# Down projections of three groups as seven half-size products for each pair of output tiles

## The reference

```python
h = rms_norm(x, g_mlp[layer])
x = x + jnp.square(jax.nn.relu(h @ w_up[layer])) @ w_down[layer]
```

## Time and profile before

| | us |
|---|---|
| median of 3 runs | 1569.56 (1568.65 to 1571.38) |
| the profiled execution | 1571.89 |
| its span | 1570.2 |
| TensorE busy | 1517.2 (97%) |
| VectorE busy | 726.8 (46%) |
| ScalarE busy | 491.9 (31%) |
| granted clock of TensorE, mean | 0.989 of 2.4 GHz |

### The profile page before, as it was taken

How to read it: one execution, slowest core, us unless ns; L and a number is a source line. 1 busy time by engine, 2 the same in 40 slices (tenths; PEclk the granted TensorE clock), 3 DMA queues, 4 the chain that set the end, 5 groups by cost and what they waited for, 6 DMA issues and landing times.

```text
span 1570.2 us, 33444 instructions
## 1 busy us (share of the span) xinstructions
PE 1517.2 (97%) x13119; PEld 1423.2 (91%) x13119; DVE 726.8 (46%) x1265; ACT 491.9 (31%) x787; POOL 117.8 (8%) x238
## 2 busy tenths in 40 slices
PE   6999999989999999999999999898999999999996
PEld 5999867679999999999999996666999999999996
DVE  4355475635443343333543466764544434334333
ACT  5111254423332131221321116442333313213133
POOL 5310112310000000000010000222000000000000
PEclk9999999999999999999999999999999999999998
DMA  4322577732223222232242237775223222322222
GB/s 132 98 80 79 151 245 251 257 101 82 79 80 94 80 80 82 79 94 81 80 136 80 82 101 238 241 236 163 75 81 87 81 83 78 94 80 81 83 79 74
DMA packets 230949, 178.84 MB, mean 114 GB/s; under 512 B 9320, under 2 KB 202924, under 8 KB 230850
## 3 DMA queue, kind: packets, MB, share of 16 engines
q1 hardware_dynamic: 217154, 137.50, 29.9%
q0 software_dynamic: 13696, 40.00, 8.0%
HBM read 170.20 MB, written 7.26 MB: 113 GB/s over the span
## 4 chain that ended last, share of the span: by engine, by line
PE 91%; DVE 3%; SPq 2%; issue 1%; DMA 1%; ACT 1%; POOLq 0%; POOL 0%; ACTq 0%; DVEq 0%
PE B L1301 70%; PE B L1518 4%; PE B L1530 3%; PE B L1327 2%; PE B L1612 2%; PE B L1574 1%; PE B L1318 1%; PE B L1550 1%; PE B L1561 1%; SPq L382 1%; DMA WR<-in_w_in_even_dram 1%; DVE SK L1194 1%; PE B L1596 1%; PE B L1528 1%; PE B L1400 1%
## 5 line engine op out<-in xcount | busy, mean ns | idle before, releaser
L554 ACT ACTIVATE WH<-WR 128x1024 fp32r<-128x1024 f32 x175 | 184.3, 1053 | 435.1 <-PE B L1301 422.3
L822 DVE TENSOR_TENSOR WL<-WR,WH 128x1024 fp32r<-128x1024 f32 x188 | 230.2, 1224 | 57.8 <-ACT WH L544 29.0
L1301 PE MATMUL B<-ffH,WH 128*128 128x288 f32 x1024 | 219.7, 295 | 0.0
L1301 PE MATMUL B<-ffL,WH 128*128 128x288 f32 x1024 | 218.0, 294 | 0.0
L1301 PE MATMUL B<-ffH,WL 128*128 128x288 f32 x1024 | 217.5, 293 | 0.0
L1301 PE MATMUL B<-H2H,WH 128*128 128x288 f32 x960 | 205.7, 294 | 0.0
L1301 PE MATMUL B<-H2L,WH 128*128 128x288 f32 x960 | 204.2, 294 | 0.0
L1301 PE MATMUL B<-H2H,WL 128*128 128x288 f32 x960 | 203.8, 293 | 0.0
L1301 PE MATMUL B<-HH,WH 128*128 128x288 f32 x832 | 179.4, 297 | 4.1 <-DVE WL L822 2.6
L1301 PE MATMUL B<-HH,WL 128*128 128x288 f32 x832 | 178.1, 296 | 0.0
L856 DVE TENSOR_TENSOR X<-B,X 128x288 f32 (+1 forms) x160 | 65.9, 453 | 242.4 <-PE B L1301 242.1
(11 more groups left out here) (297 smaller groups left out, 1692.4 us busy)
## 6 DMA issues: line engine op xcount, KB each, us to landing
WR<-in_w_up_dram SPq DMA_DIRECT2D x64, 512.0 KB, 4.1
WR<-in_w_down_dram SPq DMA_DIRECT2D x64, 512.0 KB, 3.7
KRX<-in_cache_fox_k_dram SPq DMA_DIRECT2D x48, 256.0 KB, 4.2
WR<-in_w_in_odd_dram SPq DMA_DIRECT2D x24, 512.0 KB, 3.7
...
```

The source lines that it names most:

```text
L554: A(WH[1 - u][:], WR[1 - u][:], ACT.Copy).then_inc(S["w_high"], 1)
L822: V.tensor_tensor(WL[u][:], WR[u][:], WH[u][:].bitcast(F32), ALU.subtract).then_inc(S["w_low"], 1)
L1301: last = M(B[2 * u + h][:, 0:TH], w[u][:, k, :], x[:, k, h * TH:(h + 1) * TH], start=(k == 0 and n == 0), stop=(k == KT - 1 and n == 2))
```

## The change

The hidden tiles of groups 0, 1 and 2 are no longer kept as ffH and ffL. The down projection of such a group goes over NQ=4 pairs of output tiles. A pair's product is a 2x2 block product: blocks of weights by output tile m and parity e of the k tile (a11, a12, a21, a22, each [128, 4, 128]), blocks of activations by parity of the hidden tile and half of the tokens. It is made of seven block products instead of eight (Winograd's form): of weights a11, a12, a22 and the sums S1 = a21+a22, S2 = S1-a11, S4 = a12-S2, S3 = a11-a21, with the activation blocks 11, 21, 22 and the differences T1, T2, T3, T4. Each product is 4 k tiles x 3 terms = 12 matmuls of 288 columns into one bank, of all eight in turn, and is added with its operand broadcast to one, two, three or four quarters of the pair's two tiles of X.

- The order becomes up 0, seven 0, up 1, seven 1, up 2, seven 2, up 3, down 3. The loops over down units of groups 0 to 2 are gone.
- `evac_ops` evacuates an up unit to FR; an odd unit (u=1) also makes T2, T3, T4, an even one T1; ScalarE copies to OPH, VectorE subtracts to OPL.
- SP loads the weights of a pair (1 MB) into ZR or WRP by turns; ZR, ZH, ZL, ZS lie on HH and HL, WRP on WR[0] and WR[1].
- For each pair ScalarE makes seven ZH (`block_high`) and VectorE four sums (`weight_sum`), seven ZL (`block_low`) and seven additions (`add_product`). Pair 0's are put among the last two up units, the others among the additions of the pair before.
- The first unit of down 3 waits for the last hidden tile only ahead of its last k tile (`late_chunk_unit`).
- Several semaphores are merged (f_ln, tok_scale, state_turned and others); this is left out below, as are empty lines. Indents are reduced within a piece.

```diff
+OPH = place("OPH", [P, 7, KT // 2, TH], F32R, arena)
+OPL = place("OPL", [P, 7, KT // 2, TH], F32R, arena + 14 * KT * TH)
+FR = place("FR", [P, 8, TH], F32, arena + 28 * KT * TH)
+ZH = place("ZH", [P, 7, KT // 2, P], F32R, h_addr)
+ZL = place("ZL", [P, 7, KT // 2, P], F32R, h_addr + 14 * KT * P)
+ZS = place("ZS", [P, 7, KT // 2, P], F32, h_addr + 14 * KT * P)
+ZR = place("ZR", [P, KT, 2 * P], F32, h_addr + 28 * KT * P)
+WRP = place("WRP", [P, KT, 2 * P], F32, wr_addr)
+SC = place("SC", [P, 2, KT // 2, P], F32, tmp_addr)
...
+MLP_ORDER = [("up", 0), ("seven", 0), ("up", 1), ("seven", 1), ("up", 2), ("seven", 2), ("up", 3), ("down", 3)]
+NQ = KT // 2
+OP_T1, OP_11, OP_21, OP_22, OP_T2, OP_T3, OP_T4 = range(7)
+FR_T1, FR_11, FR_12, FR_21, FR_22, FR_T2, FR_T3, FR_T4 = range(8)
+PRODUCTS = [("11", OP_11), ("S1", OP_T1), ("12", OP_21), ("S2", OP_T2), ("S4", OP_22), ("S3", OP_T3), ("22", OP_T4)]
+SUM_NO = {"S1": 1, "S2": 2, "S4": 3, "S3": 4}
+def pair_no(L, grp, q):
+    return (L * (FG - 1) + grp) * NQ + q
+def product_bank(q, i):
+    return B[(4 + 7 * q + i) % 8]
...
+def block_src(Q, i):
+    name = PRODUCTS[i][0]
+    if name in ("S1", "S2"):
+        return SC[:, int(name[1]) - 1]
+    if name in ("S3", "S4"):
+        return ZS[:, i]
+    return raw_block(Q, int(name[0]) - 1, int(name[1]) - 1)
+def up_loop(eng, body, g0, i0, turns):
+    with eng.Fori(0, turns) as it:
+        for u in range(2):
+            body(it * 2 + (g0 + u), it * 2 + (i0 + u), it + i0 // 2, u, "next")
...
+if kind == "seven":
+    for q in range(NQ):
+        Q = pair_no(L, grp, q)
+        if q == 0 and grp == 0:
+            sp.wait_ge(S["unit_done"], G_OUT[L] + KT + 1)
+        if q == 1:
+            sp.wait_ge(S["w_low"], g + 2)
+        if Q >= 2:
+            sp.wait_ge(S["block_low"], 7 * (Q - 1))
+        sp.dma_start((ZR if q % 2 == 0 else WRP)[:, :, :], dn_v[L][grp][:, :, 2 * P * q:2 * P * (q + 1)]
+                     ).then_inc(S[f"pair_in{q % 2}"], 16)
+    sp.wait_ge(S["block_low"], 7 * (pair_no(L, grp, NQ - 1) + 1))
+    continue
...
+def evac_ops(L, grp):
+    m0 = L * FG * KT + grp * KT
+    j0 = pair_no(L, grp, 0)
+    def body(g, i, j, u, more):
+        next_high(g, u, more)
+        act.wait_ge(S["relu_scaled"], i + (m0 + 1))
+        raw = FR[:, FR_11:FR_12 + 1] if u == 0 else FR[:, FR_21:FR_22 + 1]
+        A(raw, raw, ACT.Square).then_inc(S["relu_squared"], 1)
+        if u == 1:
+            act.wait_ge(S["relu_squared"], i + (m0 + 1))
+            A(OPH[:, OP_21:OP_22 + 1, ds(j, 1), :].rearrange("p s o t -> p (s o) t"), raw, ACT.Copy).then_inc(S["op_high"], 1)
+        act.wait_ge(S["op_sums"], j * 3 + (3 * j0 + 1 + 2 * u))
+        lo, hi, f = (OP_T1, OP_11, FR_T1) if u == 0 else (OP_T2, OP_T4, FR_T2)
+        A(OPH[:, lo:hi + 1, ds(j, 1), :].rearrange("p s o t -> p (s o) t"), FR[:, f:f + hi + 1 - lo], ACT.Copy).then_inc(S["op_high"], 1)
+    return body
+def block_high(Q, i):
+    name = PRODUCTS[i][0]
+    if name in SUM_NO:
+        act.wait_ge(S["w_sum"], 4 * Q + SUM_NO[name])
+    else:
+        act.wait_ge(S[f"pair_in{Q % 2}"], 16 * (Q // 2 + 1))
+    if Q >= 1:
+        act.wait_ge(S["product"], 7 * (Q - 1) + i + 1)
+    A(ZH[:, i], block_src(Q, i), ACT.Copy).then_inc(S["block_high"], 1)
...
+if kind == "seven":
+    for q in range(1, NQ):
+        for i in range(7):
+            block_high(pair_no(L, grp, q), i)
+    cut_high(g)
+    continue
+if kind == "down":
     for i in range(KT):
         evac_sq(2 + 2 * L)(g + i, i, i % 2, None if last and i == KT - 1 else "next")
+elif grp == FG - 1:
+    unit_loop(act, evac_up(L, grp), g, KT)
 else:
-    body = evac_up(L, grp) if kind == "up" else evac_none
+    body, Q = evac_ops(L, grp), pair_no(L, grp, 0)
     if n == 0:
         next_high(g, 0, "second")
         norm(1 + 2 * L)
-        body(g, 0, 0, None)
-        body(g + 1, 1, 1, None)
+        body(g, 0, 0, 0, None)
+        body(g + 1, 1, 0, 1, None)
     first = 2 if n == 0 else 0
-    unit_loop(act, body, g + first, KT - first, i0=first)
+    up_loop(act, body, g + first, first, (KT - 2 - first) // 2)
+    block_high(Q, 0)
+    block_high(Q, 1)
+    body(g + KT - 2, KT - 2, NQ - 1, 0, "next")
+    for i in range(2, 5):
+        block_high(Q, i)
+    body(g + KT - 1, KT - 1, NQ - 1, 1, None)
+    block_high(Q, 5)
+    block_high(Q, 6)
...
+def evac_ops(L, grp, b0=0, z=None):
+    m0 = L * FG * KT + grp * KT
+    j0 = pair_no(L, grp, 0)
+    def body(g, i, j, u, more):
+        next_low(g, u, more)
+        if z is not None and u == 0:
+            norm(z)
+        dve.wait_ge(S["unit_done"], g + 2)
+        f0 = FR_11 if u == 0 else FR_21
+        for h in range(2):
+            done = V.scalar_tensor_tensor(FR[:, f0 + h], B[b0 + 2 * u + h][:, 0:TH], 0.0, R[:, h * TH:(h + 1) * TH], ALU.max, ALU.mult)
+        done.then_inc(S["relu_scaled"], 1)
+        dve.wait_ge(S["relu_squared"], i + (m0 + 1))
+        if u == 0:
+            V.tensor_tensor(FR[:, FR_T1], FR[:, FR_12], FR[:, FR_11], ALU.subtract).then_inc(S["op_sums"], 1)
+        else:
+            V.tensor_tensor(FR[:, FR_T2], FR[:, FR_22], FR[:, FR_T1], ALU.subtract).then_inc(S["op_sums"], 1)
+            V.tensor_tensor(FR[:, FR_T3], FR[:, FR_22], FR[:, FR_12], ALU.subtract)
+            dve.wait_ge(S["op_sums"], j * 3 + (3 * j0 + 2))
+            V.tensor_tensor(FR[:, FR_T4], FR[:, FR_21], FR[:, FR_T2], ALU.subtract).then_inc(S["op_sums"], 1)
+            low_ops(OP_21, OP_22, FR_21, j, j * 3 + (3 * j0 + 2)).then_inc(S["op_half"], 1)
+        lo, hi, f = (OP_T1, OP_11, FR_T1) if u == 0 else (OP_T2, OP_T4, FR_T2)
+        low_ops(lo, hi, f, j, j * 3 + (3 * j0 + (1 if u == 0 else 3))).then_inc(S["evac_dve"], 1)
+    return body
+def low_ops(lo, hi, f, j, made):
+    dve.wait_ge(S["op_high"], made)
+    return V.tensor_tensor(OPL[:, lo:hi + 1, ds(j, 1), :].rearrange("p s o t -> p (s o) t"), FR[:, f:f + hi + 1 - lo],
+                           OPH[:, lo:hi + 1, ds(j, 1), :].rearrange("p s o t -> p (s o) t").bitcast(F32), ALU.subtract)
+def block_low(Q, i):
+    dve.wait_ge(S["block_high"], 7 * Q + i + 1)
+    V.tensor_tensor(ZL[:, i], block_src(Q, i), ZH[:, i].bitcast(F32), ALU.subtract).then_inc(S["block_low"], 1)
+def weight_sum(Q, q, name):
+    a11, a12, a21, a22 = (raw_block(Q, m, e) for m in range(2) for e in range(2))
+    out = block_src(Q, [o[0] for o in PRODUCTS].index(name))
+    if name == "S1":
+        dve.wait_ge(S[f"pair_in{q % 2}"], 16 * (Q // 2 + 1))
+        done = V.tensor_tensor(out, a21, a22, ALU.add)
+    elif name == "S2":
+        dve.wait_ge(S["w_sum"], 4 * Q + 1)
+        done = V.tensor_tensor(out, SC[:, 0], a11, ALU.subtract)
+    elif name == "S4":
+        if Q >= 1:
+            dve.wait_ge(S["product"], 7 * (Q - 1) + 5)
+        dve.wait_ge(S["w_sum"], 4 * Q + 2)
+        done = V.tensor_tensor(out, a12, SC[:, 1], ALU.subtract)
+    else:
+        if Q >= 1:
+            dve.wait_ge(S["product"], 7 * (Q - 1) + 6)
+        done = V.tensor_tensor(out, a11, a21, ALU.subtract)
+    done.then_inc(S["w_sum"], 1)
+def add_product(Q, q, i):
+    dve.wait_ge(S["product"], 7 * Q + i + 1)
+    if i > 0:
+        dve.wait_ge(S["product_read"], 7 * Q + i)
+    bank = product_bank(q, i)[:, 0:TH]
+    both = X[:, 2 * q:2 * q + 2, :]
+    if i == 0:
+        x = both.rearrange("p m (h t) -> p m h t", h=2)
+    elif i == 1:
+        x = both[:, :, TH:T]
+    elif i == 3:
+        x = both.rearrange("p m t -> p (m t)")[:, TH:2 * T].rearrange("p (n t) -> p n t", t=TH)
+    elif i == 5:
+        x = X[:, 2 * q + 1, :].rearrange("p (h t) -> p h t", h=2)
+    else:
+        x = {2: X[:, 2 * q, 0:TH], 4: X[:, 2 * q, TH:T], 6: X[:, 2 * q + 1, 0:TH]}[i]
+    if i == 0:
+        bank = bank.unsqueeze(1).unsqueeze(1).broadcast_to([P, 2, 2, TH])
+    elif i in (1, 3, 5):
+        bank = bank.unsqueeze(1).broadcast_to([P, 3 if i == 3 else 2, TH])
+    V.tensor_tensor(x, bank, x, ALU.add).then_inc(S["product_read"], 1)
...
+if kind == "seven":
+    for q in range(NQ):
+        Q = pair_no(L, grp, q)
+        for i in range(7):
+            if q < NQ - 1 and i in (0, 1, 4, 5):
+                weight_sum(Q + 1, q + 1, {0: "S1", 1: "S2", 4: "S4", 5: "S3"}[i])
+            add_product(Q, q, i)
+            if q < NQ - 1:
+                block_low(Q + 1, i)
+            elif i == 5:
+                cut_low(g, 0)
+    continue
+if kind == "down":
     for i in range(KT):
         evac_add(2 + 2 * L)(g + i, i, i % 2, None if last and i == KT - 1 else "next")
+elif grp == FG - 1:
+    unit_loop(dve, evac_up(L, grp), g, KT)
 else:
-    body = evac_up(L, grp) if kind == "up" else evac_add(None)
+    body, Q = evac_ops(L, grp), pair_no(L, grp, 0)
     if n == 0:
         for u in range(2):
-            evac_up(L, grp, 4, 1 + 2 * L)(g + u, u, u, "second" if u == 0 else None)
+            evac_ops(L, grp, 4, 1 + 2 * L)(g + u, u, 0, u, "second" if u == 0 else None)
     first = 2 if n == 0 else 0
-    unit_loop(dve, body, g + first, KT - first, i0=first)
```

(71 more changed lines are left out.)

46 lines of the change are left out of this document (25 added, 21 removed).

## The result

The changed kernel took **1616.01 us** in the median of four runs (1612.59 to 1618.98), against 1570.47 us for the kernel before in the same rounds (1568.65 to 1573.94). The ratio is 1.0285, with a 95% interval of 1.0263 to 1.0307. The profiled span is 1613.8 us, 43.6 us above the one before. The forecast was 1611 us.

A forecast was written before the change was run, and what follows sets the result against it. TensorE was taken to bound the kernel, busy 97% of the span. Waits net of removed matmuls (+21 us) and low clock (+20 us) on the 1569.6 us median gave 1611 us, range 1585 to 1640.

The forecast's parts named there:

- Removed, 38.1 us: Down projections of three groups in two layers: 48 matmuls fewer each, 6 x 6.35 = 38.1 us saved.
- Steps of 0.60 us for 512 elements: VectorE: operations behind one another overlap, so each of 512 elements costs 0.60 us, not its full 0.684.
- rival B: VectorE's pieces take their full duration, 13.6 us for a pair, 28 us more in all: 1639 us; chance 0.10.
- Broadcast PSUM operand at 1.04 ns for an element: VectorE's additions into X: no traced operation had this operand, so the rate of 1.04 ns an element was taken.
- Odd units 0.2 us, first groups 1.1 us: Up units: TensorE waits 0.2 us behind an odd unit, twice a group; 1.1 us in each layer's group 0.
- Last up unit stands 3.9 us: Unit 7's weight cut stands behind six VectorE operations for pair 0, so TensorE waits 3.9 us; six groups: 23.4 us.
- Rival E: Unit 7's cut isn't behind the sums, because VectorE gets to them earlier: 1578 us; chance 0.05.
- Third product 0.7 us: Product "12" wants unit 7's 576-element subtraction, which ends at 3.8 us against 3.17: TensorE stands 0.7 us.
- A pair takes VectorE 12.1 us, the seam 49.6 us, TensorE stands 4.1 to 4.6: VectorE lags TensorE's 11.1 us a pair; the next up weights load late, 49.6 us from last to next up unit.
- Rival D: VectorE keeps pace with TensorE in the seven products and the seam costs nothing: 1561 us if clock holds; chance 0.04.
- The clock, 20 us: Behind each of TensorE's twelve stands a 3.3 us half-clock stretch loses 1.65 us: 20 us, bounds 0 to 41.
- Rival C: Low-clock stretches as long as the one at 328.7 (6.8 us): 12 x 1.7 us more, 1631 us; chance 0.15.

The follow-up runs named there:

- woven: Changed kernel with unit 7's cut before the sums, fourth pair loaded to FR's place and cut earlier, pair 0's work woven into units 5 to 7: 1544.30 us.
- both_more: 36 unused VectorE subtractions added to the changed kernel with unit 7's cut first and fourth pair in FR's place, next cut earlier (1559.19 us): 1580.58 us.
- both_less: Sums S3 and S4 left out of the changed kernel with unit 7's cut first and fourth pair in FR's place, next cut earlier (1559.19 us): 1547.88 us.
- cut7_first: Changed kernel with the cut of unit 7's weights moved ahead of pair 0's weight sums and low halves: 1582.40 us, ratio 1.006 to the kernel before.
- pool_sums: Changed kernel with the four weight sums of each pair made by GpSimd instead of VectorE: 1588.22 us, ratio 1.0102 to the kernel before.
- pair3_late_cut: Changed kernel with the fourth pair loaded to FR's place, the next up group's first cut left behind the sixth addition: 1605.44 us.
- filled: Changed kernel with 24 unused dummy matmuls in each of TensorE's twelve stands: 1587.16 us, ratio 1.0099 to the kernel before.

## Why the prediction was right

The mechanism held at every place: both waits stand where they were put, for the reasons given, twelve in all and all on the cut, and nothing else grew. Some sizes were off, in two directions that cancelled.

- **Removed, 38.1 us.** 288 matmuls fewer on the page, and `woven` shows that they can be won when nothing else stands in the way: it keeps 28 us of them.
- **Steps of 0.60 us for 512 elements.** Right. The six starts above are 0.60 apart, also between operations that wait for a semaphore that is already set. That decides against rival B, and against the rule of the Trainium skill as quoted there, for these shapes; the same section of "VectorE: DVE Perf Modes" adds that an operation that is not held starts earlier, which the forecast left out. `both_more` gives 0.54 to 0.59 for the step a second time, as time of the whole kernel.
- **Broadcast PSUM operand at 1.04 ns for an element.** Right: 1152 elements by this rate are 1.20, and with the 0.15 us of a single instruction 1.35; the group took 1352 ns.
- **Odd units 0.2 us, first groups 1.1 us.** 0.26 for an odd unit: 38.59 for six units with two odd waits in `both_less`, against 38.08. The other 0.27 of 38.86 comes with the first matmuls behind a stand, a term that the forecast did not have (up 3, without odd waits, takes 51.04 against 50.77). A first group waited 0.42.
- **Last up unit stands 3.9 us.** 3.6. The six sums and lows and the cut were read rightly; the queue started a little earlier than counted. `cut7_first` shows the cause to be the place in the queue. Rival E is out.
- **Third product 0.7 us.** 0.45.
- **A pair takes VectorE 12.1 us, the seam 49.6 us, TensorE stands 4.1 to 4.6.** The rows below give 458.87-447.04 = 11.83 us for a pair; the load took 4.25 against 4.0, and the way from the last up unit to the next up unit 488.97-440.21 = 48.8 us. TensorE stood 3.48. The order of cause was right: VectorE behind TensorE, so the last low late, so the load late. Rival D needed a pair below 11.1 us; what it said of the seam came true where VectorE kept pace (0.48 us in `pool_sums`). But the working treated the load as the only wait; `pair3_late_cut` shows that the queue behind it would have held the cut for nearly as long (2.95 us).

The chain in the products, first additions of two pairs, and the busy time in the products of group 0 (columns as in the earlier trace rows: PE, PEld, VectorE, ScalarE, GpSimd):

```profile
447.04 1.27 DVE X L1055
458.87 1.27 DVE X L1055
```
```profile
442.00:487.00 45.00, 43.04 (x324) 42.60 (x322) 43.06 (x67) 15.43 (x26) 0.00 (x0) 1.00 0.23 68
```

VectorE works for 43.06 of 45 us there, as long as TensorE.

- **The clock, 20 us.** About 30: 28.9 by `filled`, 30.4 by the durations. This is the term that was mis-sized. The step that failed is "I take a low stretch of 3.3 us behind each": ten of twelve were of 6.8 us, of which a part of each lay in the stand, so a stretch cost 2.5 us and not 1.65. The rows of before show one of each length, and its four stretches were two of each; I took the shorter. Rival C's lengths were right for ten of twelve, its price was too high, since it counted them whole.

Without the clock the stands and the smaller terms came to 12 to 13 us over the time before by the rows (`filled`, with one low stretch left, is 16 above it), not 21; with the clock at 30 and not 20 the two errors cancel to within 5 us. The number 1611 against 1616 looks better than its terms are.
